# Two-layer hybrid attention decoder, float32: the order of the prompt's score matrix products of two heads

## The reference

```python
# compressed / selected / window branches of the 8 NSA heads: plain masked softmax
p = masked_softmax(einsum('btghd,bsgd->bghts', q, k) * scale, mask)
# forgetting attention, 4 heads: a term of the forgetting sums is added to the scores
s = (einsum('bthd,bshd->bhts', q, k) * dh**-0.5
     + cum_q[..., :, None] - cum_k[..., None, :])
p = masked_softmax(s, pos_k <= pos_q)
o = einsum('bhts,bshd->bthd', p, v)
```

## Time and profile before

| what | value |
|---|---|
| median of 3 runs | 3373.79 us (3373.24 to 3378.26) |
| profiled execution, first to last instruction | 3368.1 us |
| TensorE busy | 3184.9 us, 95% |
| VectorE, ScalarE, GpSimd busy | 606.5, 400.6 and 149.5 us |
| mean granted clock of TensorE | 0.960 |
| attention, layer 1 | 385 to 805 us, then the rest of stick-breaking |
| attention, layer 2 | 2034 to 2453 us, likewise |

### The profile page before, as it was taken

One profiled execution on the slowest core, in us unless ns is written; L12 is line 12 of the kernel. 1 busy time (PEld: TensorE's weight loads), 2 busy tenths in 40 slices (PEclk: granted clock), 3 DMA queues, 4 the chain that ended last, 5 costly groups with the idle time before them and its releaser, 6 DMA issues.

```text
span 3368.1 us, 40659 instructions
## 1 busy us (share of the span) xinstructions
PE 3184.9 (95%) x14318; PEld 2384.8 (71%) x14318; DVE 606.5 (18%) x1254; ACT 400.6 (12%) x924; POOL 149.5 (4%) x236
## 2 busy tenths in 40 slices
PE   6999999998799999999999999999989999999997
PEld 5878744454488878888878795444446888888886
DVE  2111244411000110000020214443110111100002
ACT  1010022112211010000011001221122010000000
POOL 0000011111000000000000001111100000000000
PEclk9999999988899999999999999998989999999998
DMA  5342132233322122212413321331432222122120
GB/s 165 123 89 66 51 92 89 73 91 98 101 60 76 67 75 75 75 60 69 135 61 101 85 70 57 96 94 45 128 94 85 75 75 72 54 75 75 52 86 26
DMA packets 304829, 272.80 MB, mean 81 GB/s; under 512 B 59282, under 2 KB 274498, under 8 KB 304370
## 3 DMA queue, kind: packets, MB, share of 16 engines
q1 hardware_dynamic: 287826, 260.55, 25.6%
q10 hardware_dynamic: 16800, 9.61, 1.0%
HBM read 260.48 MB, written 17.97 MB: 83 GB/s over the span
## 4 chain that ended last, share of the span: by engine, by line
PE 90%; DVE 3%; issue 2%; ACT 2%; SPq 1%; POOL 1%; DMA 0%; ACTq 0%; POOLq 0%; DVEq 0%
PE ps L551 18%; PE ps L552 18%; PE ps L1006 9%; PE ps L651 7%; PE ps L522 6%; PE ps L588 5%; PE ps L589 5%; PE ps L698 3%; PE ps L857 3%; PE ps L929 3%; PE ps L737 2%; PE ps L924 1%; PE ps L848 1%; PE ps L765 1%; PE ps L769 1%
## 5 line engine op out<-in xcount | busy, mean ns | idle before, releaser
L551 PE MATMUL ps<-hT,ring 128*128 128x260 f32 x2176 | 657.6, 384 | 10.4 <-DVE hT L1301 10.4
L552 PE MATMUL ps<-hT,ring 128*128 128x260 f32 x2176 | 656.4, 383 | 0.0
L551 PEld LDWEIGHTS ps<-hT,ring 128*128 128x128 f32 x2176 | 414.9, 191 | 75.1 <-DVE hT L1301 11.2
L552 PEld LDWEIGHTS ps<-hT,ring 128*128 128x128 f32 x2176 | 414.9, 191 | 64.3
L1006 PE MATMUL ps<-PT,ring 128*128 128x260 f32 x1408 | 309.1, 383 | 1.7 <-DVE PT L1581 1.7
L1006 PEld LDWEIGHTS ps<-PT,ring 128*128 128x128 f32 x1408 | 267.4, 190 | 43.5 <-issue 2.5
L651 PE MATMUL ps<-arena,ring 128*128 128x127 f32 (+1 forms) x1024 | 238.8, 407 | 0.0
L588 PE MATMUL ps<-hT,ring 128*128 128x260 f32 x704 | 215.4, 388 | 13.2 <-DMA ring<-in_w_in 8.1
L651 PEld LDWEIGHTS ps<-arena,ring 128*128 128x128 f32 x1024 | 209.7, 206 | 24.4
L589 PE MATMUL ps<-hT,ring 128*128 128x260 f32 x704 | 214.2, 386 | 0.0
L551 PE MATMUL ps<-PT,ring 128*128 128x260 f32 x512 | 158.4, 392 | 7.9 <-DVE PT L1572 4.5
(11 more groups left out here) (243 smaller groups left out, 2505.3 us busy)
## 6 DMA issues: line engine op xcount, KB each, us to landing
ring<-in_w_in SPq DMA_DIRECT2D x20, 2048.0 KB, 8.2
units<-in_cache_fox_kv SPq DMA_DIRECT2D x256, 128.0 KB, 2.2
units<-in_cache_sb_kv SPq DMA_DIRECT2D x256, 128.0 KB, 2.2
ring<-in_w_ffn_gate SPq DMA_DIRECT2D x22, 1024.0 KB, 5.4
ring<-in_w_ffn_up SPq DMA_DIRECT2D x22, 1024.0 KB, 7.9
ring<-in_w_ffn_down SPq DMA_DIRECT2D x16, 1408.0 KB, 6.3
units<-in_cache_nsa_cmp_kv SPq DMA_DIRECT2D x128, 128.0 KB, 2.2
units<-in_cache_nsa_sel_kv SPq DMA_DIRECT2D x256, 64.0 KB, 1.8
```

The source lines that it names most:

```text
L551: mm(ps[:, b, 0:H2], w, a[:, 0:H2], start=k == 0, stop=k == n - 1)
L552: last = mm(ps[:, b + 1, 0:H2], w, a[:, H2:T], start=k == 0, stop=k == n - 1)
```

## The change

All of it is inside `scores` on TensorE. Where the calls for head 0 were all issued before those for head 1, the products of both heads now come first, then, in fox items, the forgetting terms of both, then the masks of both. Operands, banks, flags, waits and the increment of `s_ps` on the last mask are as they were.

```diff
+                w = NCP if br == "cmp" else (i + 1) * P
                 for hh in range(2):
                     r = slice(hh * DH, (hh + 1) * DH)
-                    o = ps[:, hh, :]
-                    q = PT[r, qt, i * P:(i + 1) * P]
+                    keys = ckP[r, 0, 0:NCP] if br == "cmp" else PT[r, {"sel": SELK, "win": WINK, "fox": FXK + idx - 4}[br], 0:w]
+                    mm(ps[:, hh, 0:w], PT[r, qt, i * P:(i + 1) * P], keys, start=True, stop=True, skip_group_check=True)
+                if br == "fox":
+                    for hh in range(2):
+                        h = 2 * (idx - 4) + hh
+                        mm(ps[:, hh, 0:w], C("onehot", 4)[:, h * P:(h + 1) * P], ncum[:, 0:w], start=False, stop=True, skip_group_check=True)
+                for hh in range(2):
                     if br == "cmp":
-                        mm(o[:, 0:NCP], q, ckP[r, 0, 0:NCP], start=True, stop=True, skip_group_check=True)
-                        last = mm(o[:, 0:NCP], identb, mcmpb[:, i * 32:i * 32 + NCP], start=False, stop=True, skip_group_check=True)
-                        continue
-                    kt = {"sel": SELK, "win": WINK}.get(br) or FXK + idx - 4
-                    w = (i + 1) * P
-                    mm(o[:, 0:w], q, PT[r, kt, 0:w], start=True, stop=True, skip_group_check=True)
-                    if br == "fox":
-                        h = 2 * (idx - 4) + hh
-                        mm(o[:, 0:w], C("onehot", 4)[:, h * P:(h + 1) * P], ncum[:, 0:w], start=False, stop=True, skip_group_check=True)
-                    last = mm(o[:, i * P:w], identb, mcausal, start=False, stop=True, skip_group_check=True)
+                        last = mm(ps[:, hh, 0:w], identb, mcmpb[:, i * 32:i * 32 + NCP], start=False, stop=True, skip_group_check=True)
+                    else:
+                        last = mm(ps[:, hh, i * P:w], identb, mcausal, start=False, stop=True, skip_group_check=True)
                 last.then_inc(sems["s_ps"], 1)
```

## The result

The changed kernel takes 3281.26 us, the median of 4 runs (3279.93 to 3282.12), against 3373.51 us for the kernel before (4 runs): a ratio of 0.9725, 95% interval 0.9711 to 0.9739. That is 92 us less.

The account below looks back on a forecast made before the run. TensorE, busy 95% of the span, was taken as the bound. 83.4 us saved less 11.7 of waits, plus 3.4, less 10 for the clock, gave 65 net: span 3303, plus 5.7 carried over, 3309 us; range 3295 to 3347.

Parts of the forecast that it names:

- X + 0.09: Sel and win items: saving to the last mask, X being one product step, 1.06 us at width 512.
- the 83.4: Attention, both layers: TensorE time saved in us, from sel and win 53.1, cmp 13.8 and fox 16.5.
- side by side at full speed: Both heads' products in attention run at once on separate row halves, saving a whole product step; chance 0.68.
- the row of column strips: L929 in the earlier trace: 16 passes into two strips took 2.73 us, not 3.41, taken as evidence for overlap.
- the rival's price for the pair: Attention products one after the other: second costs its passes only, 0.20 us saved a pair; kernel 3346 us, chance 0.14.
- The 5 us that the prediction put on it: Fox items: saving that the forgetting terms would lose if loads for the same rows were not hidden.
- The term of 11.7 us: Attention turns, both layers: saved time that becomes TensorE's waiting for GpSimd, 5.9 us a layer.
- the floor: Turns in attention: 0.13 us from GpSimd's end to the turn's start, where TensorE already waits; 13 turns a layer.
- three more pieces of 3.4 us at 1.2 GHz a layer: Attention: added half-clock time as products take a smaller share, each piece costing 1.7 us, -10 in all.
- the rival below: Slower, by the clock: attention's mean clock falls to about 0.84 or less; at 0.80 kernel takes 3399 us; chance 0.05.
- -10 + 3.4: Attention, both layers: 10 us lost to added half-clock pieces, 3.4 gained as items already at 1.2 GHz save double.
- 5.7 us: Whole kernel: amount by which the median of runs lies above the profiled span, carried over to the forecast.

Follow-up runs that it names:

- same_rows: Changed kernel, but both heads' products read rows 0 to 63, so they can't lie side by side; 3331.1 us, ratio 0.9884.
- Full_rows_new: Changed kernel, but each product of sel, win, fox and cmp reads all 128 rows; 3307.2 us, ratio 0.9813.
- before_filler: Kernel before, with six useless products of 128 rows and 128 columns in front of each item; 3400.4 us, ratio 1.0088.
- before_four_changes: Kernel before, with four one-column products of 4, 128, 4 and 128 rows in front of each item; 3429.3 us, ratio 1.0167.
- masks_together: Kernel before, with head 1 reversed to mask, term, product, so that the masks are neighbours but the products are not; 3359.0 us, ratio 0.9961.
- four_changes: Changed kernel, with four one-column products of 4, 128, 4 and 128 rows in front of each item's products; 3315.2 us, ratio 0.9819.
- fox_old: Changed kernel, with the old order kept in the 16 fox items; 3310.2 us, ratio 0.9806.
- split_before: Kernel before, with the scaling of the second head's probabilities moved from GpSimd to VectorE; 3346.1 us, ratio 0.9912.

## Why the prediction came out as it did

**TensorE's own time was right.** The item of width 512 takes 1.13 us to its last mask instead of 2.27 (X + 0.09 = 1.15 was the saving), the fox item of that width 3.05 instead of 4.37 at full clock (the item at 796.25 in the timeline of before; 1.35 reckoned, 1.32 measured). Item by item over both traces, each from its first product to the instruction behind it with time at 1.2 GHz counted half, the saving is 82 us, so the 83.4 stand within 2%. The likeliest case, side by side at full speed, is the one that happened, and the row of column strips in the earlier trace rows was the right one to go by; same_rows gives the rival's price for the pair to 0.01 us.

**The two rules of the Trainium skill.** "TensorE: Matmul & The Clock Gate", section "Measured speedup vs the span model", has four row strips at 3.07 times the speed. Two row strips here show no slowdown: 1.06 us for one and for two; four were not tried. The passage "What overlaps and what doesn't" of the same page (section "The mechanism") would have left the loads of the second forgetting term exposed. The four passes of width 512 take 1.91 us (720.83 to 722.74), which is four times 0.427 and one load and change of shape: the other loads are hidden though they go to the same rows. The trace disagrees with that rule. The 5 us that the prediction put on it were too many even so: 16 pairs at 0.20 are 3.2.

**The waits were mis-sized.** The term of 11.7 us measured 19 (2 x 9.5). The turns were picked well: compared one by one, 17 turns of a layer wait in this stretch, 13 of them those that stood at the floor before. But the 13 alone wait 6.1 us longer a layer. Each pays the whole saving of the next scores, 0.42 or more, also where the turn before it had waited, and the sum took that part off: three in a row (544, 549 and 554 us in the kernel after) pay 0.42, 0.42 and 0.52. Four turns that before started 0.3 to 0.95 us behind GpSimd's end add 2.2, and ScalarE's copy, called untouched, 0.9. The mechanism was as told, and it cost 7 us more.

**The step that failed is the clock.** The prediction put "three more pieces of 3.4 us at 1.2 GHz a layer", -10, because products "take a smaller share afterwards". Its bounds were called "0 and the rival below", both on the slow side, so a clock that rises was left out of the sum and of the range. Time at 1.2 GHz in attention went down by 48 us in both layers (58.0 to 34.1 each) instead of up by 20. TensorE was busy in 46 of them, worth 23 us (half of it), where -10 + 3.4 stood in the sum. Outside these stretches there are 7.2 us more: 2.7 are the last item of each layer, and some 4 are left, where the time at 1.2 GHz fell by another 11 us. The sum is then 82 - 19 + 23 + 4 = 90, and the two spans say 88.5; where the 2 us lie I can't say. The reasoning took the products for the dense part of a long stretch. My reading now is the reverse: a product of 64 rows used half the array's rows, alone, and was followed by an empty piece, so what was taken out was the thin part, and the rest of the work, unchanged, came closer together. Full_rows_new against same_rows (0.968 and 0.964) and before_filler against before_four_changes, with the length held, speak for it; same_rows and masks_together show that the gain comes in steps with each shortening, with no overlap needed. That the clock rose is shown; why it rose is argued from these runs. What I can't give is a rule that says how much: four_changes should have cost more clock if thinness were all, and it cost 0.002.

**A smaller slip: what lies around the span.** I carried over 5.7 us from the profiled span to the median. Each run of the kernel after lists its own span, and the difference is 1.9 us every time (3281.49 and 3279.6). The other 3.8 were that the profiled execution of the kernel before was a quick one: its clock was 0.960, while the median over the 17 runs beside fox_old was 0.957 with times from 3366.7 to 3382.3. That put the forecast 4 us too high.

Together: 30 for the clock inside attention, 4 outside it, 4 for the carry, less 7 for the waits and 1 for the work, make 30, where the miss is 28 us.

**What else could have been known.** The runs of before beside the experiments spread over 8 to 16 us a set with the clock from 0.955 to 0.961, while the changed kernel's four stay within 2.2. A kernel whose equal runs differ so much by their clock has time to win or lose there, and split_before shows how much: a move that was to save 10 us of waits brought 31.

## What to carry to other kernels

Where two products each read half the rows of the array and write different banks, issue them as direct neighbours: they run at once, and a single column of anything in another shape between them undoes it. Group small products by the rows they read, since each change of shape cost 0.09 us and exposed a weight load of 0.11. And where part of a TensorE-bound stretch runs at the lower clock, don't charge a saving for making the stretch sparser before asking what the removed time held, and leave room in the range for a clock that rises: taking out products of half the rows and the empty time behind them raised it here, and a saving of some 64 us net of waits became 88.

## What the hardware showed that I had not expected

- The same 0.43 us added to each item moved the run's granted clock from 0.958 to 0.9605 with full products and to 0.952 with one-column products that change shape, 29 us apart, with equally little idle time of TensorE.
- Two row strips in two banks cost nothing beside each other: 1.06 us for two float32 products of 512 columns, as for one.
- A float32 product of 512 columns and 128 rows takes 0.91 to 0.96 us between masks, less than the 1.06 of one with 64 rows, since 64 rows bring a change of shape.
- Identical executions of the kernel before spread from 3364.9 to 3382.3 us, in step with their clock (0.961 to 0.955); those of the changed kernel, four runs, from 3279.9 to 3282.1.
